# RWKV's low-rank products made over all 128 rows, with zeros in the other direction's half, the rotary tables moved, and new orders for the mixers' streams

## The reference, cut to what matters

```python
y_a = hgrn2_mixer(a_q, a_ff, a_fb, a_i, ...) * silu(a_g)      # H
y_b = retention_mixer(b_q, b_k, b_v, ...) * silu(b_g)         # B
y_c = rwkv7_mixer(c_s, ...) * silu(c_g)                       # R, its inputs P
mixed = gates[0]*(y_a @ w_branch_a) + gates[1]*(y_b @ w_branch_b) + gates[2]*(y_c @ w_branch_c)
x = x + mixed @ w_out
```

```python
for d in range(2):
    w = w0[d] + tanh(w_code[:, :, d]) @ w_lora_b[d]     # 64 -> 1024
    a = sigmoid(a0[d] + a_code[:, :, d] @ a_lora_b[d])  # 64 -> 1024
    k_d = k * (1.0 + (a - 1.0) * k_a)
    o = o + rwkv7_scan(r, exp(-exp(-softplus(-w) - 0.5)), k_d, v, kk, a, reverse=(d == 1))
    bonus = bonus + sum(r * k_d * r_k) * v
y = head_groupnorm(o, ln_g, ln_b) + bonus
```

## Time and profile before

| what | value |
|---|---|
| three runs | 3051.78, 3057.10, 3058.19 us |
| median | 3057.1 us |
| the profiled execution | 3052.44 us; its span 3050.6 us |
| TensorE: mean granted clock | 0.994 |
| busy | PE 2976.8 us, PEld 2456.9, DVE 1662.9, ACT 709.3, POOL 258.9 |
| DMA | 395.56 MB, mean 130 GB/s |

### The profile page before, as it was taken

The page is one execution under the profiler, slowest core; times in us unless marked ns, Lnnn a source line. Parts: engine busy times, 40 slices in busy tenths (PEclk is TensorE's granted clock), DMA queues, the critical chain, the costliest instruction groups (busy, mean ns, idle before and its releaser), DMA issues.

```text
span 3050.6 us, 45196 instructions
## 1 busy us (share of the span) xinstructions
PE 2976.8 (98%) x18944; PEld 2456.9 (81%) x18944; DVE 1662.9 (55%) x3430; ACT 709.3 (23%) x1344; POOL 258.9 (8%) x319
## 2 busy tenths in 40 slices
PE   8999999999999999999999999899989999999999
PEld 7888888888886887888888887795859869766894
DVE  2667566456321555766646611675247667645674
ACT  2343334234101333332334310200021010013100
POOL 1111302102100021210210200000000000000000
PEclk9999999999999999999999999999999999999999
DMA  6333323333244432333324235454334445432453
GB/s 226 101 113 103 117 97 100 114 119 119 81 161 137 136 101 83 97 114 127 103 84 146 86 120 187 132 173 166 138 110 166 166 158 173 167 113 109 151 169 122
DMA packets 153755, 395.56 MB, mean 130 GB/s; under 512 B 90289, under 2 KB 106801, under 8 KB 109649
## 3 DMA queue, kind: packets, MB, share of 16 engines
q1 hardware_dynamic: 51376, 367.94, 34.5%
q10 hardware_dynamic: 100608, 19.93, 3.2%
q0 software_dynamic: 1568, 4.79, 0.5%
HBM read 380.04 MB, written 12.59 MB: 129 GB/s over the span
## 4 chain that ended last, share of the span: by engine, by line
PE 91%; DVE 4%; DMA 2%; ACT 1%; issue 1%; POOL 0%; ACTq 0%; DVEq 0%; SPq 0%
PE bank L418 28%; PE bank L2016 18%; PE bank L1839 7%; PE bank L2034 7%; PE bank L435 7%; PE bank L1902 4%; PE bank L1443 2%; PE bank L2045 1%; DMA rw_direction<-scores_scratch 1%; PE bank L1011 1%; PE bank L759 1%; PE bank L779 1%; PE bank L1725 1%; PE bank L1025 1%; PE bank L892 1%; PE bank L1103 1%
## 5 line engine op out<-in xcount | busy, mean ns | idle before, releaser
L418 PE MATMUL bank<-h_features,weight_ring 128*128 128x256 f32 x4192 | 955.7, 382 | 1.9 <-DVE h_features L531 1.0
L418 PEld LDWEIGHTS bank<-h_features,weight_ring 128*128 128x128 f32 x4192 | 783.6, 190 | 121.1 <-issue 14.9
L435 PE MATMUL bank<-weight_ring,h_features 128*128 128x256 f32 (+1 forms) x896 | 204.4, 379 | 0.8 <-ACT rt_qk L1742 0.8
L435 PEld LDWEIGHTS bank<-weight_ring,h_features 128*128 128x128 f32 x896 | 164.0, 190 | 26.4 <-ACT rt_qk L1742 2.8
L2016 PE MATMUL bank<-h_features,weight_ring 128*128 128x128 f32 x1408 | 172.0, 275 | 6.1 <-DVE h_features L531 6.1
L2016 PEld LDWEIGHTS bank<-h_features,weight_ring 128*128 128x128 f32 x1408 | 164.3, 192 | 6.9 <-DVE h_features L531 6.9
L2087 ACT COPY mem_normed<-bank 128x128 f32<-128x128 f32 x88 | 23.3, 265 | 482.2 <-PE bank L2016 476.6
L1839 PE MATMUL bank<-y_features,weight_ring 128*128 128x256 f32 x512 | 121.0, 386 | 0.0
L2172 DVE TENSOR_TENSOR mem_normed<-mem_normed,bank 128x256 f32<-128x256 f32 x88 | 37.1, 421 | 131.1 <-PE bank L2016 131.1
L1839 PEld LDWEIGHTS bank<-y_features,weight_ring 128*128 128x128 f32 x512 | 94.0, 190 | 13.9 <-issue 1.3
L2016 PE MATMUL bank<-h_features,y_features 128*128 128x128 f32 x704 | 93.0, 275 | 0.0
(11 more groups left out here) (543 smaller groups left out, 4876.0 us busy)
## 6 DMA issues: line engine op xcount, KB each, us to landing
weight_ring<-in_w_in SPq DMA_DIRECT2D x146, 1024.0 KB, 5.0
weight_ring<-in_f00w SPq DMA_DIRECT2D x33, 1024.0 KB, 4.9
weight_ring<-in_f01w SPq DMA_DIRECT2D x33, 1024.0 KB, 4.8
weight_ring<-in_f10w SPq DMA_DIRECT2D x33, 1024.0 KB, 4.8
weight_ring<-in_f11w SPq DMA_DIRECT2D x33, 1024.0 KB, 4.8
weight_ring<-in_w_b SPq DMA_DIRECT2D x16, 1024.0 KB, 4.8
weight_ring<-in_w_out SPq DMA_DIRECT2D x16, 1024.0 KB, 4.9
weight_ring<-in_conv_in SPq DMA_DIRECT2D x10, 1024.0 KB, 4.8
```

The costliest lines, as they stand in the source:

```text
L418: m = e.matmul(bank[:, j, :], w[:, k, j * P:(j + 1) * P], x[:, k, :], start=k == 0, stop=k == kt - 1, skip_group_check=True)
L435: m = e.matmul(bank[:, t * n:(t + 1) * n], x[:, k, t * P:(t + 1) * P], w[:, k, :], start=k == 0, stop=k == kt - 1, skip_group_check=True)
```

## The change

- The four LoRA weights of a quarter (two codes, two directions) get a tile of their own each, 128 x 256. It holds the direction's 64 rows at their old place, and zeros in the other 64 rows. The zeros are written once by GpSimd at the start of the kernel; the first LoRA product waits for them.
- The LoRA product multiplies all 128 rows of that tile with all 128 rows of `codes` (64 of one direction, 64 of the other; the zeros take the other's away).
- A quarter's LoRA loads are four DMAs of 64 rows instead of two of 128. The semaphore counts follow.
- The rotary tables' tile (1280 bytes a row) moves from the tiles of the whole kernel to those of the second block, where it takes space that the mixers' tiles had.
- All the `ORDER` strings of the two mixers stages are new: tensor, vector, scalar, gpsimd and sync. Every stream has the same steps as before.

The strings, cut (both layers have the same ones; start and end of the tensor string, the gpsimd string in full, the start of the sync string):

```diff
     ("mixers0", "tensor"):
-        "R P4 H2 P4 H2 P4 H2 P5 H P H P H4 P2 H P H P2 H P H3 R P H R H3 B R B R B R4 B2 H P4 B4 H2 B P R H2 R3 P "
...
-        "H R4 H9 B4 R B R3 B R2 B2 R2 B R B R B R2 B2 R4 H R2 H2 R H R H R2 H R2 H R2 H6 R9 H13 R29 ",
+        "R P4 H2 P4 H2 P4 H2 P5 H P H P H4 P2 H P H P2 H P H4 R P H3 B R B2 R B2 H R B R4 B H2 P4 B3 H2 B P R P "
...
+        "R19 H19 ",
     ("mixers0", "gpsimd"):
-        "H R4 H10 R2 H6 R2 H11 R2 H5 R H3 R H7 R2 H6 R2 H17 R ",
+        "H R4 H12 R2 H4 R2 H11 R2 H5 R2 H8 R2 H8 R3 H17 ",
     ("mixers0", "sync"):
-        "P H P2 H P H3 B2 P B P3 B3 H5 B P B2 P2 B P B2 H3 B3 H2 B3 P B6 P2 H P2 H4 B10 H3 B2 H2 B H R2 H3 R7 ",
+        "P H P2 H P H3 B2 P B P3 B3 H5 B4 P3 B P B H2 B2 H B H2 P B P B2 P3 H B6 H3 B2 H B9 R3 B2 R H4 R5 H5 ",
```

The code:

```diff
@@ -627,7 +627,7 @@
     R.inputs = [[R(f"{n}{i}", *for_t) for n in ("r", "k", "v", "kk")] + [R(f"vt{i}", TT, 2 * P)] for i in range(2)]
     R.bonus, R.o = [R(f"bonus{i}", *for_t) for i in range(2)], R("o", TT, 2 * P)
     R.a, R.kd = R("a", *for_t), R("kd", *for_t)
-    R.lora = [R("lora_w", 2 * P), R("lora_a", 2 * P)]
+    R.lora = [[R(f"lora_{n}{d}", 2 * P) for d in range(2)] for n in "wa"]
     R.rhs, R.w, R.ktok, R.atok = (R(n, 2 * P) for n in ("rhs", "w", "ktok", "atok"))
     R.state = R("state", 2, P)
     R.scored_a, R.scored_k = R("scored_a", TT, 4, 2, P), R("scored_k", TT, 4, 2, P)
@@ -886,11 +886,12 @@
         for free in g.banks.free("lora", l, q, d, code):
             e.wait_ge(*free)
         if d == 0 and code == 0:
-            e.wait_ge(g.lora_sem, 32 * (4 * l + q + 1))
+            e.wait_ge(g.lora_sem, 64 * (4 * l + q + 1))
+            e.wait_ge(*g.st.pool.at("lora"))
             e.wait_ge(*g.cd.act.at("tanh", l))
         for n in range(2):
-            m = e.matmul(bank[:, n, :], R.lora[code][d * 64:(d + 1) * 64, n * P:(n + 1) * P],
-                         g.codes[d * 64:(d + 1) * 64, code, :], start=True, stop=True, skip_group_check=True)
+            m = e.matmul(bank[:, n, :], R.lora[code][d][:, n * P:(n + 1) * P], g.codes[:, code, :], start=True,
+                         stop=True, skip_group_check=True)
         m.then_inc(*S.pe.up("lora", l, q, d, code))
     yield
 
@@ -1224,7 +1225,9 @@
 
 def lora_pool(e, g, l, q):
     for i, lora in enumerate(("lora_w", "lora_a")):
-        e.dma_start(g.R.lora[i], g.t[f"{lora}{l}"][:, 2 * q * P:2 * (q + 1) * P]).then_inc(g.lora_sem, 16)
+        for d, rows in enumerate(ROW_HALVES):
+            e.dma_start(g.R.lora[i][d][rows], g.t[f"{lora}{l}"][rows, 2 * q * P:2 * (q + 1) * P]).then_inc(
+                g.lora_sem, 16)
 
 
 def doublings_dve(e, g, l, q, d):
@@ -3066,6 +3069,8 @@
     zeros = g.R.scored_a.rearrange("p c h s t -> p (c h s t)")
     e.memset(g.nm_one, 1.0).then_inc(*g.st.pool.up("one"))
     e.memset(g.R.state, 0.0).then_inc(*g.st.pool.up("state"))
+    for z in (z for code in g.R.lora for z in code):
+        e.memset(z, 0.0).then_inc(*g.st.pool.up("lora"))
     e.memset(zeros, 0.0).then_inc(*g.st.pool.up())
     e.wait_ge(*g.st.pool.now())
     for t in (g.x_scratch, g.xT_scratch):
@@ -3141,9 +3146,6 @@
         self.nm_sq = flat(self.yc3[:, 4:8, :])
         self.nm_ss, self.nm_one = sb("norm_sum", TT)[:, :], sb("norm_one", 1)[:, :]
         self.pos_i = sb("positions", TT, I32)[:, :]
-        rope = sb("rope", 5 * TT * 32)[:, :]
-        self.cos_t, self.sin_t, self.rope_ang, self.rope_n, self.rope_r = (
-            view(rope[:, i * 64:(i + 1) * 64], (TT, 32)) for i in range(5))
         with ExitStack() as stage:
             rwkv_tiles(self, stage)
             hgrn_tiles(self, stage)
@@ -3151,6 +3153,9 @@
         with ExitStack() as stage:
             keep = Tiles(self, stage, "ff")
             self.act_t, self.silu = keep("act", FT, T), keep("silu", 2, T)
+            rope = keep("rope", 5 * TT * 32)
+            self.cos_t, self.sin_t, self.rope_ang, self.rope_n, self.rope_r = (
+                view(rope[:, i * 64:(i + 1) * 64], (TT, 32)) for i in range(5))
             self.final_gain = flat(self.act_t[:, 0:4, :])
             self.v = keep("mla_v", TT, MIX)
             self.k_rope_gain, self.q_rope_gain = keep("k_rope_gain", QR), keep("q_rope_gain", QR)
```

## The result

The changed kernel takes 3034.9 us (median of four executions, 3032.4 to 3036.9) where the kernel before takes 3057.6 in the same sitting (3051.8 to 3066.7). The ratio is 0.9929, 95% interval 0.9912 to 0.9946: 22 us less, 17 to 27. Forecast were 3049, within 3038 to 3063. One execution of a later kernel ("Both", 3357 us at a mean clock of 0.865) is left out of its times, and its trace isn't used.

A forecast was written before the change was run, and what follows sets the result against it. TensorE, busy 98% of the span, was taken as the bound. Terms -7.4 - 2.6 - 1.1 - 1.4 - 1.7 + 1.4 + 5 gave -7.8 us, from the median 3057.1 to 3049, range 3038 to 3063.

The forecast's parts named there:

- the clock: TensorE's mean granted clock of 0.994: 18 us lost at 1.2 GHz; half-speed stretches only put in the spread, some us either way.
- The change of shape: TensorE around LoRA products: 19 fewer changes between 64-row and 128-row tiles per layer, 38 at 0.195 us, -7.4 us.
- rival 3: LoRA product L892: half-row passes might cost 0.142 us, so full rows add 9.5 us, sum +1.7, 3059; chance 0.05.
- GpSimd's queue: Added memsets and 16 more LoRA load issues on GpSimd: taken as 0, bounds 0 and 8.6 us.
- Waits that stay or go: TensorE's mixer waits under the new order: L802 -2.6, L1101 -1.1, L1443 -1.4, bonus product -1.7 us.
- the +1.4: End of each layer's mixers, before w_out: one more addition behind the last product, 0.73 us per layer, +1.4 us.
- the bonus product: L1128, 12.9 us in 7 waits: first, second and last quarters' waits stay, the third quarter's shrink, -1.7 us.
- Unseen new waits: TensorE waits that the new order brings and the trace can't show: +5 us, bounds 0 and 10.
- rival 2: Scratch round trip to the loaded inverse: late replies cost some 6 us per unit; four give +16, 3073; chance 0.10.
- Rival 1: Mixers: TensorE comes sooner to steps others release and waits there; unseen waits 10, sum -2.8, 3054; chance 0.30.

The follow-up runs named there:

- Both: Changed kernel, with GpSimd clearing score tiles only after the bonus operand and w_out waiting slice by slice: 3018.3 to 3031.9 us; second set 3019.2 us, ratio 0.9871.
- the last kernel: Changed kernel with later clearing, w_out by slices, and one retention projection step moved ahead of L759 in each layer: 3013.0 us, 0.9857 of the kernel before.
- the kernel before without both waits: Kernel before (old orders, half-row LoRA), with clearing only after the bonus operand and w_out waiting slice by slice: 3027.7 us, ratio 0.9909.
- the four waits added: Changed kernel with later clearing, w_out by slices, and an input projection step moved ahead of L759, shifting ten steps: 3048.0 us, 0.9976 of the kernel before.
- taking one of the two waits alone: Two kernels, each the changed kernel with one edit: clearing only after the bonus operand, 3026.0 us; w_out waiting slice by slice, 3032.1 us.

## Where the prediction was right and where it was wrong

Two steps of the prediction failed. One is that it gave the clock no term ("some us either way"): it was worth 7 to 8 us. The other is that it summed the change in waits to -0.4 us: the trace after has 6.3 us less. The rest held to within some 2 us.

- *The change of shape* (-7.4): right in mechanism, somewhat too large. L893 takes 0.215 a pass, and passes fell by 4.9 to 6.6 us between the two kernels, 5.5 to 7.1 in the old order for 38 changes, 7.5 in the new for 44: 0.13 to 0.19 each. I had priced all of them from LoRA steps that stood alone. (The Trainium skill, TensorEngine Tiling (Array Packing), Key Properties, says that a change of the tiling mode drains TensorE and gives no time; the runs agree so far as each change costs time, by these numbers.)
- *A half-row pass could be cheap* (rival 3): fell. Between the passes inside a LoRA step, where no shape changes on either side, it is 0.216 us from start to start over 64 rows (before) and over 128 (after).
- *GpSimd's queue* (0, bounds 0 and 8.6): right in the new order, where no wait at L1446 is left; in the old one it cost 3 to 4. The bound was worth stating.
- *Waits that stay or go*: L802 and L1101 went as worked out (-2.6, -1.1), w_out's grew by 1.6 for the +1.4. Three were missed. L1443 lost all seven waits, not only its longest (2.8 for 1.4). L1011 and L770 (2.2) I had left out of the sum. And the bonus product lost 3.9, not 1.7: I had kept its wait in the last quarter because as much work lies between as before. But what stops VectorE there is GpSimd's clearing, and where that stands in GpSimd's queue I hadn't looked up. Before, GpSimd was done with HGRN and cleared at once (its timeline, kernel before):

```profile
846.26 1.80 POOL L1221 MEMSET rw_scored_a<- 128x2048 f32 x1 [68.46 <-PE bank L1103]
```

After, RWKV's last quarter ends before HGRN's, and the clearing stands behind HGRN's levels; PE's and GpSimd's timelines:

```profile
794.49 1.03 PE L1129 MATMUL bank<-rw_bonus,float_constants 128*128 128x256 f32 x4
```

```profile
801.67 0.61 POOL L1662 TENSOR_TENSOR hg_ks<-hg_bf 128x256 f32<-128x256 f32 x1 [24.01 <-PE bank L1446]
...
830.46 1.82 POOL L1222 MEMSET rw_scored_a<- 128x2048 f32 x1
```

- *Unseen new waits* (+5): 3.9 at L759, 0.5 at L418, 0.3 at L435, 4.7 in all. The guess from the old plan's own chance waits held. Its largest is rival 2's scratch trip in kind, in each layer's first unit, at a third of that rival's price.
- *Rival 1, the plan gives it back*: fell; 6.3 us of waiting went.
- *The clock*: this step failed most. I read 0.994, worked out 18 us, and then gave it no term, only "some us either way". It was worth 3 to 10 us between traces; by the executions' mean clocks, in the median 0.993 against 0.9955 over 3050 us, 7 to 8. Two things that I had on the table belonged together: the waits of the earlier trace rows and the low stretches. I counted them from the first mixers stage to the end of the second one's w_out, in the twelve traces ahead of the last kernel's. There are 42 low stretches; 41 begin in a wait of PE of 1.35 us or more or within 3.5 us behind it. The other way about, 41 of 82 such waits have one, and their length matters: 2 of 21 below 1.7 us (twelve of the 21 are one and the same wait, at the norm between the two layers, that never has one), 39 of 61 above. A low stretch of 3.4 us costs 1.7 us, so over all 82 a wait costs its length and about 1.1 us more on average. That it is the waits and not something that goes with them is shown by the kernel before without both waits, by the four waits added, and by the last kernel. Which of the longer waits gets one isn't known: two executions of one kernel differ in it, and taking one of the two waits alone gave no clock back.

With the clock at 7 and the missed waits at 6, the sum would have been -7.8 - 7 - 6 = -21, or -19 with the changes of shape as measured, against -22. These two are fitted afterwards and are no second prediction.

## What to carry to other kernels

Where TensorE is 98% busy, as here, list each of its waits with what its granted clock does in the next few us, and price the waits together with both; a single one may give back its own length alone. When an order changes, ask for each stall that contention causes where the other engine's instruction now stands in its own queue. And a step that is moved within a stream moves all steps between: take the nearest one that passes none of its own.

## What the runs showed of the hardware

- Waits of 1.4 to 5.3 us of a TensorE that was otherwise busy had 3.4 us or more at 1.2 GHz in or behind them in half of the cases (41 of 82). Six stretches were of 10.2 or 13.7 us: four cover rounds of 64x64 products, two begin in waits of 5.3 us.
- A kernel had a stretch of 27.3 us at half speed in one traced execution (13.7 us of time), and two of its other executions took 17 to 18 us less.
- One VectorE tensor_scalar stood still through two successive clearings on GpSimd (3.38 us in place of 0.33 to 0.35).
- A change of tile shape costs 0.39 us there and back around a LoRA step of 256 columns; averaged over what the change removed, 0.13 to 0.19 for one.
